# Hybrid attention layer on eight cores: score matmuls of two key steps in one group, and a rotation by transfers

## What is computed

```python
q = rms_norm(q.reshape(b, n, 8, 2, 64), q_norm_w); k = rms_norm(k..., k_norm_w)
q, k = apply_rope(q, cos, sin), apply_rope(k, cos, sin)      # latent tokens only
# apply_rope: a1, a2, b1, b2 = split(x); rot = concat([-a2, a1, -b2, b1]); x * cos + rot * sin   (pieces of 16 channels)
k_all = concat([cache_k, k]); v_all = concat([cache_v, v])
s = einsum("bqhcd,bkhcd->bhcqk", q, k_all) * 64 ** -0.5; p = softmax(s)
a = p[:, :, 0] - lam * p[:, :, 1]; o = rms_norm(a @ v_all, subln_w) * (1 - lam_init)
# then: spatial gating of the two other streams, output projection, MLP of width 8192, each with gated residuals
# outputs: y_prompt, y_sample, state_k and state_v (keys and values of the prompt tokens)
```

## Time and profile before

| | us |
|---|---|
| three runs: lowest, median, highest | 2718.28, 2721.84, 3072.1 |
| profiled execution: its own time | 2717.43 |
| its span, slowest core (core 2) | 2716.4 |
| spans of all cores | 2704.2 to 2716.4 |
| granted TensorE clock, mean of each core | 0.978 to 0.984 |
| PE busy in the span | 2491.7 (92%) |
| ACT busy, DVE busy | 844.7 (31%), 965.7 (36%) |

### The profile page before, as it was taken

The page is one execution under the profiler, slowest core; times in us unless marked ns, Lnnn a source line. Parts: engine busy times, 40 slices in busy tenths (PEclk is TensorE's granted clock), DMA queues, the critical chain, the costliest instruction groups (busy, mean ns, idle before and its releaser), DMA issues.

```text
span 2716.4 us, 57279 instructions; the slowest of 8 cores (2704.2 to 2716.4 us)
## 1 busy us (share of the span) xinstructions
PE 2491.7 (92%) x22177; PEld 1757.3 (65%) x22177; DVE 965.7 (36%) x2368; ACT 844.7 (31%) x1700; POOL 233.8 (9%) x362
## 2 busy tenths in 40 slices
PE   1378999999998889998999999999999999999999
PEld 1345555565565544476586786867885876868768
DVE  0253433443443330665142331423452332413324
ACT  1445666556656651644101001010032001010010
POOL 0111111111111010002000000000010000000000
PEclk9989999999999889999999999999999999999999
DMA  9995334324333367164666666667966666666667
GB/s 182 223 198 102 55 58 81 64 49 81 64 56 68 61 103 117 20 147 72 107 97 106 97 106 98 106 97 142 200 124 109 97 106 97 106 98 106 97 106 157
DMA packets 82153, 282.42 MB, mean 104 GB/s; under 512 B 11424, under 2 KB 44896, under 8 KB 58336
## 3 DMA queue, kind: packets, MB, share of 16 engines
q0 software_dynamic: 43232, 226.87, 52.9%
q1 hardware_dynamic: 38656, 51.89, 6.3%
HBM read 488.78 MB, written 16.81 MB: 186 GB/s over the span
## 4 chain that ended last, share of the span: by engine, by line
PE 82%; ACT 5%; DVE 4%; DMA 4%; issue 3%; another core or an unknown queue 1%; POOL 0%; DVEq 0%; ACTq 0%; POOLq 0%; SPq 0%
PE pg L1192 8%; PE pS L1192 8%; PE pO L1192 8%; PE pg L1164 8%; PE pS L1164 8%; PE pO L1164 8%; PE pO L887 5%; PE pg L622 4%; PE pS L741 3%; PE pT L622 2%; DMA arena<-w_adaA 2%; PE pg L639 2%; PE pS L1120 2%; ACT arena L868 2%; PE pO L1120 2%
## 5 line engine op out<-in xcount | busy, mean ns | idle before, releaser
L868 ACT ACTIVATE arena<-pS 128x512 bf16<-128x512 f32 x578 | 312.7, 592 | 246.1 <-PE pS L741 241.2
L1180 DVE TENSOR_TENSOR arena<-arena 128x512 bf16<-128x512 bf16 (+1 forms) x256 | 91.7, 359 | 562.6 <-ACT arena L1179 562.6
L887 PE MATMUL pO<-arena 128*128 128x129 bf16 x2432 | 201.6, 228 | 11.3 <-ACT arena L868 8.1
L1063 DVE TENSOR_TENSOR hT_own<-hT_own,arena 128x256 f32<-128x256 f32 x456 | 194.1, 426 | 50.1 <-DVE arena L1062 4.9
L887 PEld LDWEIGHTS pO<-arena 128*128 128x128 bf16 x2432 | 147.6, 101 | 78.1 <-issue 77.8
L1164 PE MATMUL pg<-arena 128*128 128x256 bf16 (+1 forms) x960 | 157.5, 322 | 0.0
L1164 PE MATMUL pO<-arena 128*128 128x512 bf16 (+1 forms) x896 | 157.0, 333 | 0.0
L1192 PE MATMUL pg<-arena 128*128 128x256 bf16 x1344 | 153.6, 273 | 0.0
L1192 PE MATMUL pS<-arena 128*128 128x256 bf16 x1344 | 153.6, 273 | 0.0
L1192 PE MATMUL pO<-arena 128*128 128x256 bf16 x1344 | 153.6, 273 | 0.0
L1179 ACT ACTIVATE arena<-pg 128x512 bf16<-128x512 f32 (+1 forms) x86 | 42.4, 493 | 345.1 <-PE pg L1164 345.1
(11 more groups left out here) (244 smaller groups left out, 3726.7 us busy)
## 6 DMA issues: line engine op xcount, KB each, us to landing
arena<-w_ff POOLq DMA_DIRECT2D x84, 1024.0 KB, 9.6
shr<-w_ff POOLq DMA_DIRECT2D x44, 1024.0 KB, 9.6
arena<-w_adaB POOLq DMA_DIRECT2D x64, 512.0 KB, 8.6
arena<-w_adaA POOLq DMA_DIRECT2D x16, 1024.0 KB, 27.5
arena<-xs SPq DMA_DIRECT2D x16, 1024.0 KB, 12.4
arena<-w_in POOLq DMA_DIRECT2D x32, 512.0 KB, 9.9
arena<-w_o POOLq DMA_DIRECT2D x12, 1024.0 KB, 12.7
hT_own<-xs SPq DMA_DIRECT2D x8, 768.0 KB, 21.1
```

The source lines that it names most:

```text
L868: A("act", lambda e, t=bk[c], P=P: e.activation(out=P, in_=t[:], func=AF.Exp, scale=0.125), reads=[bkr[c]], writes=[Pr])
L887: ins = e.matmul(pO[b][:, c * 130:c * 130 + 129], lhsT=Ps[c][0][:, j * 256 + b * 128:j * 256 + b * 128 + 128], rhs=vv[p][:, kt + j, 0:129] ...
L1063: A(eng, lambda e: e.tensor_tensor(out=acc[:, ti, c], in0=acc[:, ti, c], in1=tmp, op=ALU.add), reads=[tmr, ("acc", ti, nb)], writes=[("acc ...
L1180: A("dve", lambda e, rl=rl, fc=fc, c0=c0, cn=cn: e.tensor_tensor(out=aT[:, fc, c0:c0 + cn], in0=rl[:, 0:cn], in1=rl[:, 0:cn], op=ALU.mult) ...
```

## The change

It touches the attention stage alone, in these parts.

1. **Scores of two steps.** In heads 0 to 6 the loop goes by pairs of steps (133 pairs). `s4` emits the eight score matmuls of two steps as one group into four banks (`pS0`, `pS1`, `pg0`, `pg1`), with one signal at its end; then come the values of both steps. `av_of` of the second step is put off past three units when the first step ends a block. Head 7 keeps `s_mm`.
2. **Two banks for the rest.** With `pg` given away, the projections, the sums over channels, the transposes of `finish` and the modulation share `pT0` and `pT1` (class Shared). One bank collects a projection, the other serves the requests in a queue; after a group they swap (`swap`). A request holds its bank 2 ticks before its consumer is emitted, and the next is emitted 2 ticks after that at the earliest; none is emitted in the last two units of a group.
3. **The chain.** A group is first copied to SBUF by DVE in f32 (c0_), and the chain works on the copy. The `perm` matmul is replaced by eight DMAs of SP, SBUF to SBUF, each 16 channels by 512 tokens in bf16 (16 KB); the signs went into the table of sines. c6 is posted 7 ticks after c4.
4. **Keys channel first.** `ck` is handed over transposed and goes straight into `kT` by DMA; `sk` is stored as it lies (`skT`). The transposes and copies of both are gone.
5. **Rings and order.** `PT` 8 tiles for 4, `tbf` 6 for 4, `tf` 5 for 4, `wa2` 2 for 4. Modulation units have places of their own in the order of the groups. 112 units are spread over the 19 pairs.

```diff
+                def s4(si):
...
+                    bks = [([pS.tiles[0], pS.tiles[1]], [("pS", 0), ("pS", 1)]), ([pg.tiles[0], pg.tiles[1]], [("pg", 0), ("pg", 1)])]
...
+                    def fn(e):
+                        for i in range(2):
+                            h, q0, kt, ki, n = steps[si + i]
+                            p = h % 2
+                            for j in range(2):
+                                for c in range(2):
+                                    ins = e.matmul(bks[i][0][c][:, j * 256:j * 256 + 256], lhsT=kT[p][64 * c:64 * c + 64, (kt + j) * 128:(kt + j) * 128 + 128],
+                                                   rhs=qz[p][64 * c:64 * c + 64, q0:q0 + 256], start=True, stop=True)
+                        return ins
+                    A("pe", fn, reads=rd, writes=bks[0][1] + bks[1][1])
...
+                for si in range(0, 7 * NS, 2):
+                    h = steps[si][0]
+                    b0, b1 = s_of.pop(si), s_of.pop(si + 1)
+                    P0, P1 = [], []
+                    MP.tick()
+                    for c in range(2):
+                        exp_of(b0[0], b0[1], c, P0)
+                    exp_of(b1[0], b1[1], 0, P1)
+                    late.append(lambda b1=b1, P1=P1: exp_of(b1[0], b1[1], 1, P1))
+                    want = (si % NS // 2 + 1) * FILL_UNITS // (NS // 2)
+                    n_u = 0
+                    while 0 <= filled[h + 1] < want:
+                        if not pull(h + 1):
+                            break
+                        n_u += 1
+                        if n_u == 3:
+                            run_late()
+                            MP.tick()
+                    run_late()
+                    s4(si + 2)
+                    MP.tick()
+                    xt_()
+                    av_of(si, P0)
+                    MP.tick()
+                    if steps[si][3] == steps[si][4] - 1:
+                        late.append(lambda si=si, P1=P1: av_of(si + 1, P1))
+                    else:
+                        xt_()
+                        av_of(si + 1, P1)
```

```diff
+                class Shared:
...
+                    def release(self):
+                        fn, self.held = self.held, None
+                        if fn is not None:
+                            fn()
+                            self.free = FP.t + 2
...
+                    def step(self):
+                        if self.held is not None and FP.t >= self.until:
+                            self.release()
+                        if self.held is None and self.q and FP.t >= self.free and not self.lock:
+                            emit, consume, hold = self.q.pop(0)
+                            bk = self.banks[self.pm]
+                            emit(bk)
+                            self.held = lambda: consume(bk)
+                            self.until = FP.t + hold
+
+                    def swap(self, evict):
+                        self.release()
+                        self.pm = 1 - self.pm
+                        bk = self.banks[self.pm]
+                        self.held = lambda: evict(bk)
+                        self.until = FP.t + 1
...
+                def xt_():
+                    FP.tick()
+                    X.step()
```

```diff
+                        def c0_(bk):
+                            zt, zr = st["a"] = tf.next()
+                            A("dve", lambda e: e.tensor_copy(out=zt[:], in_=bk[0][:]), reads=[bk[2]], writes=[zr])
+                            FP.post(2, c1)
+
+                        def c1():
...
+                            A("act", lambda e: e.activation(out=sq[:], in_=zt[:], func=AF.Square), reads=[zr], writes=[sqr])
+                            FP.post(2, lambda: X.req(c2, c3))
...
+                        def c4():
...
+                            for b_ in range(8):
+                                d_, s_ = 16 * b_, 16 * (b_ ^ 1)
+                                A("sp", lambda e, d_=d_, s_=s_: e.dma_start(out=rt[d_:d_ + 16, :], in_=dst[s_:s_ + 16, :]), reads=[dr], writes=[(rr, b_), rr] if b_ == 7 else [(rr, b_)], key=("rot", rr, b_))
+                            A("pool", lambda e: e.tensor_tensor(out=rs[:], in0=dst, in1=cosT[:, r0:r0 + 512], op=ALU.mult), reads=[dr, "cosT"], writes=[rsr])
+                            FP.post(7, c6)
+
+                        def c6():
...
+                            A("dve", lambda e: e.tensor_tensor(out=zt[:], in0=rt[:], in1=sinT[:, r0:r0 + 512], op=ALU.mult), reads=[(rr, b_) for b_ in range(8)] + [rr, "sinT"], writes=[zr])
...
+                            A("dve", lambda e: e.tensor_tensor(out=dst[:, c0:c0 + 512], in0=rs[:], in1=zt[:], op=ALU.add), reads=[rsr, zr], writes=[dr])
...
+                    for o in ["k1", "v1", "A", "k2", "W", "v2", "q1", "q2", "A", "v3", "k3", "v4", "A", "k4", "v0", "k0", "V", "A", "q0"]:
```

More of the change, by code:

```diff
@@ L280, in _body @@
                 vv.append(tk3(22, 130))
-                wa2 = Ring("wa2", [tk3(16, 128) for i in range(4)])
+                wa2 = Ring("wa2", [tk3(16, 128) for i in range(2)])
+                PT_more = [ar.take(512) for i in range(4)]
+                tb_more = [ar.take(512) for i in range(2)]
+                tf_more = [ar.take(512, F32)]
                 o_raw = [tk3(4, 130, F32) for c in range(2)]
@@ L509, in ada_unit @@
                     keys = [("modc2", ci, j), ("modc2", ci, j + 1)]
[L511 to L519, removed]
@@ L704, in _body @@
                 steps = [(h, q0, keys[2 * ki], ki, len(keys) // 2) for h in range(8) for (q0, keys) in BLOCKS for ki in range(len(keys) // 2)]
-                fills = {h: fill(h) for h in range(8)}
+                fills = {h: (fill2(h) if h else fill(0)) for h in range(8)}
                 filled = [0] * 9
@@ L892, in _body, with run_late @@
                         finish(h, q0)
-                assert ada_i[0] == 64
+                late = []
+                def run_late(k=9):
+                    while late and k:
+                        late.pop(0)()
+                        k -= 1
+                for si in range(0, 7 * NS, 2):
[19 more added lines that the diff above has]
+                    MP.tick()
+                    xt_()
+                    av_of(si, P0)
+                    MP.tick()
+                    if steps[si][3] == steps[si][4] - 1:
+                        late.append(lambda si=si, P1=P1: av_of(si + 1, P1))
+                    else:
+                        xt_()
+                        av_of(si + 1, P1)
+                for si in range(7 * NS, 8 * NS):
+                    MP.tick()
+                    run_late()
+                    bk, bkr = s_of.pop(si)
+                    Ps = []
+                    for c in range(2):
+                        exp_of(bk, bkr, c, Ps)
+                    xt_()
+                    xt_()
+                    if si % NS in (4, 10, 16, 22):
+                        ada_unit()
+                    s_mm(si + 1)
+                    MP.tick()
+                    av_of(si, Ps)
+                assert ada_i[0] == 64 and ada_n[0] == 64
             MODC2 = [("modc2", ci, j) for ci in range(2) for j in range(16)]
@@ L1230, in _consts @@
         if d % 32 < 16:
-            perm[d + 16, d] = -1.0
+            perm[d + 16, d] = 1.0
         else:
```

286 lines of the change are left out of this document (193 added, 93 removed).

## The result

The changed kernel takes 2898.2 us in the median of four runs (2894.8 to 2899.2), against 2720 us before: a ratio of 1.0652, 95% interval 1.0635 to 1.0669. It is 178 us slower. The forecast was 2655 us, and the range ended at 2740. In some executions the cores of one die ran at a lower granted clock and took longer; they are left out of every time and ratio here.

What follows compares the result with a forecast made beforehand. PE, busy 92% of the span, was taken as the bound. Per loop 100.3 - 8.2 - 5.9 - 3.0 + 5 + 2 + 1.0 = 91.2 us; seven loops and head 0 save 66 us: 2655 us, range 2595 to 2740.

Steps and rivals of the forecast that it cites:

- rotation and `finish` together +5 (0 to 15): DVE stands 4 to 5 us per rotated block for the transfers, delaying copies PE needs: +5 us a loop.
- I leave **1.0** (0 to 4): PE's clock: waits above 2 us become rarer, so low clock costs 1.0 us a loop instead of 3.0.
- The 3.0 us a loop: Low clock before the change: 6% of the time at half speed, half of it lost, 3.0 us per head.
- Rival (d): Rotation becomes the bound: sets land 9 to 10 us after c4, PE waits 27 us a loop; 2790 us, chance 0.13.
- The passages: Going into the 64-row form for scores and out again costs PE 0.21 us; 19 fewer a loop.
- The `bones` wait: PE's wait at the shared bank before the sums over channels, 5.9 us a loop, goes entirely.
- ACT's term: Later exponentials, and projections waiting for the bank Ln has just read: +2 us a loop (0 to 4).
- the pairs: Scores of two steps in one group: 19 groups instead of 38, -4.0 us a loop over seven loops.
- (a): New waits are small, pieces land within c6's 7 ticks, clock stays 2.4 GHz: 84.7 us a loop, 2611 us; chance 0.20.
- (b): Waits only move from the shared bank to behind c6: 95.7 us a loop, 2688 us; chance 0.18 together with (e).
- (c): Weight loads of the long score group show: 7.2 us a loop less gain, 2705 us; chance 0.09.
- (e): Queue of requests runs full, blocks come late, the head drains alone; ends as (b), chance 0.18 together with it.

Runs made afterwards that it cites:

- `perm` kernel: Changed kernel with the rotation again a permutation matmul into a shared bank instead of eight transfers: 2669 us, ratio 0.9816.
- hold 1: Changed kernel with the permutation matmul, its requests and those for the channel sums held one tick instead of two: 2642 us, ratio 0.9715.
- the kernel whose longest wait was 1.4 us: Changed kernel with the permutation matmul, requests held one tick instead of two, and four ticks instead of two after a swap: 2633 us, ratio 0.9683.

## Why the prediction was wrong

**The mechanism was in it, its price wasn't.** The step that failed is the term "rotation and `finish` together +5 (0 to 15)" and, with it, the clock's "I leave **1.0** (0 to 4)". The transfers cost 37.4 us a loop: 26.5 of waiting, where the sum had 5 and at most 15, and 10.9 of PE's own slowing, where it had 1 and at most 4. Three things went wrong in that term.

1. *The set was sized too short.* SP's issues were taken at 0.45 us each from two loads at the start of the kernel; these stand 0.61 apart, and a set took 6.6 us in quiet and 12.5 behind slabs, not 5.6. DVE waited 7.1 us for each set, not 4 to 5. Doubling the issues moved the wait by 0.53 us for each.
2. *Who stands behind DVE was counted too kindly.* I let only the copies that were due after c6 be late, by 1.7 us, and then took off for PE's own slowing. In the trace the victims are whatever happens to be queued: the small copy of `attT`, the copies of `pO`, the copies of projections, and ACT's Ln of `finish` with all exponentials behind it. PE's idle time went from 8.1 to 30.8 us a loop. Against the 4.3 of the kernel without transfers that is 4.4 us for each of the six rotated blocks.
3. *The clock was booked as a gain.* Low clock followed the long waits before, so more long waits had to bring more of it. The mean fell from 0.97 to 0.85, and PE's busy time for the same matmuls rose from 83.4 us a loop (at 0.98) to 94.3. My sum gave 2 us back here; it should have taken about 10. My way of pricing it was wrong as well: half of the time at the low clock is 19 us of a loop here and 2 in the kernel without transfers, 17 more, where PE's busy time rose by 10.9; the clock is also low while PE stands. The 3.0 us a loop for the kernel before is likely too much for the same reason: between the `perm` kernel at 0.97 and that with hold 1 at 1.00 PE's busy time differs by 2.0 us a loop.

Rival (d) named this outcome, with the right place and the right threshold (2.9 us of new waiting of PE for each rotated block; 4.4 were measured), and with a chance of 0.13. Its 27 us of waiting a loop is close to the 26.5 measured. It was priced at 2790 and not 2898 because it had no price for the low clock (10.9 a loop) and built on a loop without transfers of 83.2 us, which measured 87.7. And the range, 2595 to 2740, did not reach it: even 15 us a loop, the term's upper bound, gives only 2725.

**What was right.** Without the transfers the sum was 83.2 + 2 + 1 = 86 us a loop; the kernel without transfers measured 87.7; that is in part luck, for the terms differ. The passages: 0.54 us from scores to values for eight was forecast as 0.55. The `bones` wait of 5.9 us a loop went to 0.2, but 3.2 came back before the modulation matmuls at the same shared bank, which the sum had at nothing. ACT's term of 2 us a loop stands at 1.2 to 2.7 in the paired kernels with `perm`. Of the 28 us for the pairs, 15 to 18 arrived; PE's busy time fell by 26, and most of the difference is ACT's wait, which the sum had in another term.

**The other rivals.** (a) and (b) fall with the 4.4 us of new waiting for each rotated block. (c), the weight loads of a long score group that show, is out. "TensorE: Matmul & The Clock Gate" of the Trainium skill says in its section on packing small matmuls that loads overlap running matmuls only if they go to other rows. The trace does not agree: the loads of the second four (PEld, 503.14) began 0.13 us after those of the first, while matmuls of the same rows were running, and it was 0.54 us from the scores to the values, not 0.93. (e), a queue of requests that runs full, is out as the cause too: the kernel without transfers has the same queue and took 2636 us, and with six requests more it took 2669.

## What to carry to other kernels

A short DMA is cheap in bytes and dear in an in-order queue: what counts is the number of issues times the queue's pitch, plus the landing behind whatever slabs are on their way, and then everything that stands behind the instruction that waits. Before moving a small matmul to transfers, ask what else is in the waiting engine's queue, and post the consumer later than the slow set, not the quiet one. And book the clock with the sign of the waits: if a change adds waits of several us for TensorE, the low clock comes on top of them, here 10.9 us of a loop beside 26.5 us of idle time. Read its price from PE's busy time for the same matmuls, not from the mean clock, which also counts the time in which PE stands.

## What the runs showed of the hardware

- Small SBUF to SBUF transfers on SP's queue: 0.507 to 0.575 us of issue each in a quiet set (2.4 at most in the kernel), a pitch of 0.61, for 16 KB and for 8 KB alike, and 1.8 us to land, 8.4 at most. Behind four slabs of 512 KB a set of eight took 12.5 us instead of 6.6.
- Eight score matmuls of 64 rows by 256 columns into four banks ran two at a time with their weight loads hidden: 0.54 us to the next full-height matmul, against 0.33 for four.
- A wait of 7.1 us of TensorE was followed by half clock; in the kernel whose longest wait was 1.4 us the granted clock was 1.00 throughout the attention's window of 520 us. Sixteen transfers a set lowered the mean clock from 0.85 to 0.80 and left PE's busy time nearly as it was (95.1 us a loop for 94.3).
